# Layer 0's residual normalisation on other hooks, and the last norm's powers ahead of its pieces, in a two-layer decoder trunk on eight cores

## The chip, the cores and the metric

One Trainium2 chip, all eight NeuronCores. Each core runs the same program on its eighth of the tokens (two sequences of 4096 tokens, 8192 in all) and needs nothing from the others. The metric is device time in microseconds of the slowest core, the median of several runs.

Engines go by their profile names: PE is TensorE, DVE VectorE, ACT ScalarE, POOL GpSimd, SP SyncE, which here only issues DMAs.

## What is computed

The cut reference:

```python
x = layernorm(x, ln_in_g, ln_in_b)                 # the input norm, once
for l in range(2):
    h = x @ w_in[l] + b_in[l]                      # q k v gate_A u v_B gate_B route_A route_B
    y_a = window_attention(q, k, v, sinks[l]) * silu(gate_A)
    y_b = gelu(u) * (tril(W_s) @ layernorm(gelu(v_B)) + b_s) * silu(gate_B)
    m = sigmoid(route_A) * (y_a @ P_A[l]) + sigmoid(route_B) * (y_b @ P_B[l])
    x = layernorm(alpha * x + m @ W_out[l] + b_out[l], ln_g[l], ln_b[l])
```

The model width is 1024. Attention looks back 128 positions, the spatial gate mixes within chunks of 128.

## The kernel before, in words

Tokens are worked in tiles of 512, four blocks (j = 0 to 3) of 128. A stage is one tile in one layer. Stages come in fours: tiles 2i and 2i + 1 in layer 0, then both in layer 1, so that stage s is the first of a layer 0 pair for s % 4 = 0, the second for s % 4 = 1, and layer 1 for the rest; there are 32 (s = 0 to 31). A stage runs through these regions on PE: vb (four token-major tiles for v_B), u, gb and ga (four feature-major tiles each for u, gate B and gate A), r (sixteen tiles for the two routes, with the attention of the tile interleaved), pb (eight merge tiles with P_B, and the transposes of the next stage's input xbf into xT behind every second one), q of the next stage, pa (eight merge tiles with P_A), kv of the next stage, and then the output projection, which is emitted at the head of the next stage. All weights stream through four ring slots, one slab of 1 MB each; releasing a slab issues the load of the fourth one behind it on SP (the first uses of a slab go through POOL's queue from the float32 original, and a bf16 copy is written back by SP).

Dependences are found by the program `P.add` from keys such as ("xres", buf, j): an instruction waits for the last writer of what it reads, and for the readers of what it writes. Every engine runs its own instructions strictly in the order in which they were emitted, a DMA wait on SP included. What sets that order around the change are hooks: `run_hooks(hooks, ("u", 2))` stands behind the third u tile, and whatever was hooked there is emitted at that place, in the order of the `hook` calls. In the loop over stages (L915 to L954) the calls come in this order: third_hooks, lnin_hooks, lnin_before, resid_hooks, and region_out with its own hooks.

- `resid_hooks` (L672) works for layer 0 on the residual of the tile. The input x is loaded again into xres (`load`, a 512 KB DMA on SP), normalised by ACT (`app`, L680, an activation 128x1024), and multiplied and added to by POOL (`ln_gb`, L445, four instructions 128x512 per block). xres has two buffers, by tile parity. It is needed as late as the output projection.
- `third_hooks` (L545) multiplies and adds, on POOL, the output of the stage before last, behind each block of the output projection; for layer 1 it also issues y's DMA on SP behind vb 0, vb 1, vb 2 and u 0. The buffer is the one which the residual loads of the same stage write.
- `lnin_hooks` (L666) serves a stage before a layer 0 stage: statistics of the next tile's input blocks 2 and 3, which sit in stg, then an activation of each into xbf (`apply`). xbf is read by the transposes in pb. `ln_rstd` (L428) takes a power on POOL, `ln_bias` (L435) a small product on DVE.
- `region_mid` (L693): ACT evicts every u, gb and ga tile from PSUM; DVE multiplies uT by gbT, makes `mixed` from PSUM, and multiplies it by uT into gbT. PE's tiles take their PSUM buffer from a pool: five for these tiles ("W"), three for the scores ("S"), three for the route tiles ("A").
- `region_attn` (L762): scores (j, c) are masked by DVE (L777), their maximum taken (L780), then ACT's exponentials write Pq; POOL divides by the denominator (`norm`); `turn` transposes, `pv` multiplies.
- `region_pa` (L874): each merge tile has a product on DVE from PSUM, and a sum tRb <- tRa + tRb on DVE.
- `final_out` (L560) is the output projection of the last stage. Per block DVE adds the product, takes statistics and POOL the power f1. `finish(j)` scales on ACT, then has two POOL pieces and a DMA per half; `centre` and `scale` do the same work with two DVE instructions per half.

Of the kernel before, what the change touches and what calls it, by code (L numbers as in the profile page):

```python
# [151 lines left out]
def build(n_tok, seq_len):  # L152
# [50 lines left out]
    gb = sb("gb", [128, 6, D])  # L203
# [356 lines left out]
    def final_out(s):  # L560
# [7 lines left out]
            c = slice(h * 512, (h + 1) * 512)  # L568
            dma(eng, y_d[r0:r0 + 128, c], xres[:, buf, j, c], (("yh", j, h),), (("y", t, j, h),), ("yf", j, h))

        def finish(j, hs=(0, 1)):
            key = ("xres", buf, j)
            stt(sm[k][:, 2, j:j + 1], mv[k][:, j, 0:1], -1.0, ALU.mult, sm[k][:, 1, j:j + 1], ALU.mult,
                (("mv", k, j), ("f1", j)), (("f2", j),))
            for h in hs:
                c = slice(h * 512, (h + 1) * 512)
                d, hk = xres[:, buf, j, c], ("yh", j, h)
                act(d, d, AF.Identity, (key, ("f1", j), ("f2", j)), (hk,), bias=sm[k][:, 2, j:j + 1],
                    scale=sm[k][:, 1, j:j + 1])
                tt("pool", d, d, gb[:, gi, c], ALU.mult, (hk, ("gb", gi)), (hk,))  # L580
                tt("pool", d, d, gb[:, gi + 1, c], ALU.add, (hk, ("gb", gi + 1)), (hk,))
                put(j, h)
# [14 lines left out]
        for j in range(4):  # L597
            key = ("xres", buf, j)
            x = xres[:, buf, j, :]
            for h in range(2):  # L600
                b = next_bank("W")
                sl = slab8(so[h])
                for kc in range(8):
                    mm(ps[b][:], tRb[:, kc, j * 128:(j + 1) * 128], sl[:, kc, :], kc == 0, kc == 7,
                       RK(so[h]) + (("tRb", kc),), (("ps", b),))
                z = xres[:, buf, j, h * 512:(h + 1) * 512]
                stt(z, z, 2.0 * ALPHA, ALU.mult, ps[b][:], ALU.add, (key, ("ps", b)), (key,))
                P.add("dve", (lambda z, j, h: lambda e: e.bn_stats(out=st[:, j, 6 * h:6 * h + 6], in_=z))(z, j, h),
                      (key,), (("st", j) if h == 0 else ("st2", j),))
            P.add("dve", (lambda j: lambda e: e.bn_aggr(out=mv[k][:, j, :], in_=st[:, j, :]))(j),  # L610
                  (("st", j), ("st2", j)), (("mv", k, j),))
            ts("dve", sm[k][:, 0, j:j + 1], mv[k][:, j, 1:2], 4.0 * EPS, ALU.add, (("mv", k, j),), (("f0", j),))
            tt("pool", sm[k][:, 1, j:j + 1], sm[k][:, 0, j:j + 1], neghalf[:, 0:1], ALU.pow,
               (("f0", j), ("neghalf",)), (("f1", j),))
            if j in (1, 2):
                finish(j - 1)
        finish(2, (0,))
        centre(3, 0)
        centre(3, 1)
        scale(3, 0)  # L620
        scale(3, 1, "act")
        centre(2, 1)
        scale(2, 1)
        release(2)

    def hook(hooks, k, f):
# [36 lines left out]
        hook(hooks, ("pa", 3), lambda: apply(1))  # L663
        hook(hooks, ("pa", 6), lambda: (load(2), load(3)))

    def lnin_hooks(s, hooks):  # L666
        load, stats, apply = lnin_parts(s)
        hook(hooks, ("vb", 1), lambda: stats(2))
        hook(hooks, ("u", 2), lambda: apply(2))
        hook(hooks, ("u", 3), lambda: apply(3))  # L670

    def resid_hooks(s, hooks):  # L672
        t, l = stages[s]
# [10 lines left out]
        if s == 0:  # L684
            at = (("r", 15), ("pb", 1), ("pb", 3), ("pb", 5))
        else:
            at = (("gb", 1), ("gb", 3), ("ga", 1), ("pb", 1))
        for j in range(4):
            if s > 0:
                hook(hooks, (("u", 1), ("u", 2), ("u", 3), ("gb", 0))[j], (lambda j: lambda: load(j))(j))  # L690
            hook(hooks, at[j], (lambda j: lambda: (app(j), ln_gb(buf, j, 0)))(j))

    def region_mid(s, hooks):  # L693
# [221 lines left out]
    for s in range(NS):  # L915
# [16 lines left out]
            third_hooks(s - 1, hooks, (("gb", 0), ("gb", 2), ("ga", 0), ("ga", 2)),  # L932
                        (("ga", 0), ("ga", 2), ("r", 0), ("r", 2)))
        if is_lnin(s):
            lnin_hooks(s, hooks)
        if is_lnin(s + 1):
            lnin_before(s + 1, hooks)
        if stages[s][1] == 0:
# [92 lines left out]
```

How the kernel before makes its waits and increments, by code:

```python
        def run(ename, e):  # L99
            seen = {}
            for op in per_eng[ename]:
                waits = {}
                for d in op.deps:
                    if d.chan is None and d.eng == "pe" and ename == "pe" and op.chan is None:
                        continue
                    s, v = event(d)
                    if v > waits.get(s, (None, 0))[1]:
                        waits[s] = (s, v)
                if op.chan is not None and not self.chan_batch[op.chan] and op.ticket > 1:
                    s = csem[op.chan]
                    v = 16 * (op.ticket - 1)
                    if v > waits.get(s, (None, 0))[1]:
                        waits[s] = (s, v)
                for s, v in waits.values():
                    if seen.get(s, 0) < v:
                        e.wait_ge(s, v)
                        seen[s] = v
                ins = op.fn(e)
                if op.chan is not None:
                    ins.then_inc(csem[op.chan], 16)
                elif op.signal:
                    ins.then_inc(esem[ename], 1)
            if ename == "sp":
                for c, s in csem.items():
                    v = 16 * self.chan_count[c]
                    if seen.get(s, 0) < v:
                        e.wait_ge(s, v)
                        seen[s] = v
```

## Time and profile before

| | |
|---|---|
| median of 3 runs | 3605.0 us (3602.7 to 3606.3) |
| the profiled execution | 3604.8 us |
| its span, slowest core (core 3) | 3603.3 us |
| spans of the eight cores | 3575.7 to 3603.3 us |
| PE busy | 3410.5 us (95%) |
| DVE busy | 2318.8 us (64%) |
| ACT busy | 1824.2 us (51%) |
| POOL busy | 1401.2 us (39%) |
| chain that ended last: PE | 87% |
| chain: DMA, DVE, ACT | 6%, 3%, 1% |
| granted PE clock, core 3, mean | 0.982 |

The span is cut into stages of 103 to 130 us behind the first one. The busy time of an engine is the union of its instructions. Behind an instruction of a timeline the brackets give the time in which its engine was idle just before it, and what ended that idleness; x4 means that four like instructions were merged into the line, whose length then runs from the first one's start to the last one's end. Matmuls overlap, so the start of the next tells more than the length of one. The granted clock is the share of TensorE's full 2.4 GHz that it was given: 1.00, or 0.50 for the 1.2 GHz level.

### The profile page before, as it was taken

To read this page: it belongs to the slowest core of one execution; us is meant where nothing else is said; L and a number is where in the kernel's file an instruction comes from. 1 tells how busy PE (TensorE), PEld (TensorE's weight loads), DVE (VectorE), ACT (ScalarE), POOL (GpSimd) and SP (SyncE) were. 2 spreads that over 40 slices of the span, in tenths; PEclk is the share of its full clock that TensorE was granted. 3 is DMA by queue.
4 is the path that set the end of the run, shared out by engine and by line. 5 is a ranking of instruction groups with operands and counts; after the bars stand their busy time and mean duration, and the time that the engine had idled before them with its cause. 6 is when DMAs were issued, how large, how long until landed. Compare 5 with 4: busy or idle time off the path is not lost.

```text
span 3603.3 us, 61737 instructions; the slowest of 8 cores (3575.7 to 3603.3 us)
## 1 busy us (share of the span) xinstructions
PE 3410.5 (95%) x18320; PEld 1600.3 (44%) x18320; DVE 2318.8 (64%) x4993; ACT 1824.2 (51%) x4065; POOL 1401.2 (39%) x1295
## 2 busy tenths in 40 slices
PE   5778989999999999999999999999999999999997
PEld 2334444444444444444444444444444444444443
DVE  3445557666676676676776666766666667666667
ACT  3434445545555545655445654455654554555543
POOL 1324135442355331543334523444325542254343
PEclk9889999999999999999999999999999999999999
DMA  8784975538355344454454444544445534455433
GB/s 164 170 234 99 184 198 193 181 112 228 135 199 182 135 158 147 170 188 143 159 174 144 178 150 164 193 148 148 145 158 199 182 135 155 138 182 187 144 133 112
DMA packets 99112, 589.84 MB, mean 164 GB/s; under 512 B 11234, under 2 KB 11490, under 8 KB 42212
## 3 DMA queue, kind: packets, MB, share of 16 engines
q1 hardware_dynamic: 91012, 536.13, 42.2%
q0 software_dynamic: 7056, 49.29, 8.4%
q8 instruction: 159, 2.61, 0.3%
q14 instruction: 165, 1.35, 0.1%
q10 hardware_dynamic: 720, 0.46, 0.0%
HBM read 573.25 MB, written 61.87 MB: 176 GB/s over the span
## 4 chain that ended last, share of the span: by engine, by line
PE 87%; DMA 6%; DVE 3%; issue 1%; ACT 1%; POOL 0%; SPq 0%; DVEq 0%; POOLq 0%; ACTq 0%
PE ps L247 84%; DMA ring<-wpk 3%; PE ps L459 2%; PE ps L813 2%; DMA stg<-x 1%; DMA xres<-x 1%; DVE gbT L258 1%; ACT xT L255 1%; DMA tRb<-bs 1%; DVE nmx L780 0%; DVE ps L777 0%; DVE tRa L268 0%; DVE sm_i L268 0%; ACT L787 0%; POOL xres L258 0%
## 5 line engine op out<-in xcount | busy, mean ns | idle before, releaser
L247 PE MATMUL ps<-xT,ring 128*128 128x512 bf16 x8448 | 1967.7, 382 | 44.4 <-DMA ring<-wpk 25.0
L247 PEld LDWEIGHTS ps<-xT,ring 128*128 128x128 bf16 x8448 | 822.1, 98 | 1024.8 <-issue 105.5
L258 POOL TENSOR_TENSOR xres<-xres,gb 128x512 f32<-128x512 f32 x762 | 988.1, 1300 | 223.4 <-ACT xres L255 141.4
L258 POOL TENSOR_TENSOR Pq<-Pq,rcp 128x512 bf16<-128x512 bf16 x256 | 261.3, 1041 | 1010.2 <-DVE rcp L800 808.7
L787 ACT ACTIVATE Pq<-ps,nmx 128x128 bf16<-128x128 f32 x1024 | 371.8, 375 | 322.3 <-DVE nmx L268 320.3
L247 PE MATMUL ps<-ring,tRb 128*128 128x512 bf16 x2048 | 452.1, 381 | 19.0 <-DMA ring<-wpk 17.3
L247 PEld LDWEIGHTS ps<-ring,tRb 128*128 128x128 bf16 x2048 | 199.6, 98 | 257.9 <-issue 29.7
L247 PE MATMUL ps<-ring,xT 128*128 128x512 bf16 (+1 forms) x2048 | 304.3, 299 | 0.0
L255 ACT ACTIVATE xres<-xres,sm_p 128x1024 f32<-128x1024 f32 (+1 forms) x129 | 155.7, 1220 | 253.6 <-DVE sm_p L268 250.3
L258 POOL TENSOR_TENSOR sm_p<-sm_p,neghalf 128x2 f32<-128x2 f32 (+1 forms) x66 | 45.6, 691 | 577.9 <-DVE sm_p L262 574.8
L247 PE MATMUL ps<-gbT,ring 128*128 128x512 bf16 x1024 | 257.2, 379 | 0.0
L780 DVE TENSOR_REDUCE nmx<-ps 128x2 f32<-128x256 f32 x512 | 217.5, 425 | 54.6 <-DVE ps L777 2.3
L268 DVE SCALAR_TENSOR_TENSOR tRa<-tRa,ps 128x512 bf16<-128x512 bf16 x256 | 174.3, 681 | 120.8 <-PE ps L247 120.7
L247 PE MATMUL ps<-gaT,ring 128*128 128x512 bf16 x1024 | 230.5, 381 | 16.0 <-DVE tRa L268 14.5
L268 DVE SCALAR_TENSOR_TENSOR xres<-xres,ps 128x512 f32<-128x512 f32 x256 | 174.9, 683 | 99.2 <-PE ps L247 93.6
L247 PE MATMUL ps<-kpad,qT 128*128 128x512 bf16 x512 | 196.3, 383 | 39.5 <-DVE nmx L780 22.2
L258 DVE TENSOR_TENSOR uT<-uT,gbT 128x512 bf16<-128x512 bf16 x128 | 81.7, 649 | 225.2 <-ACT gbT L255 225.2
L255 ACT ACTIVATE xT<-ps,cs 128x512 bf16<-128x512 bf16 x256 | 186.1, 782 | 78.6 <-PE ps L459 74.9
L777 DVE COPY_PREDICATED ps<-upper,ps 128x256 f32<-128x256 uint16 x496 | 208.2, 420 | 18.2 <-PE ps L247 18.0
L255 ACT ACTIVATE xbf<-xres,sm_p 128x1024 bf16<-128x1024 f32 x64 | 79.2, 1238 | 276.3 <-DVE sm_p L268 276.3
L247 PEld LDWEIGHTS ps<-ring,xT 128*128 128x128 bf16 x2048 | 160.1, 98 | 128.2
L787 ACT ACTIVATION_READ_ACCUMULATOR Pq<-ps,nmx 128x1 f32 x1024 | 217.0, 212 | 0.0
(92 smaller groups left out, 3619.4 us busy)
## 6 DMA issues: line engine op xcount, KB each, us to landing
ring<-ws SPq DMA_DIRECT2D x371, 1024.0 KB, 5.8
ring<-wpk POOLq DMA_DIRECT2D x45, 1024.0 KB, 13.8
xres<-x SPq DMA_DIRECT2D x64, 512.0 KB, 6.8
stg<-x SPq DMA_DIRECT2D x60, 512.0 KB, 6.2
y<-xres SPq DMA_DIRECT2D x60, 512.0 KB, 4.8
ws<-ring SPq DMA_DIRECT2D x26, 1024.0 KB, 12.1
ring<-ws SPq DMA_DIRECT2D x28, 512.0 KB, 4.4
gb<-gbr SPq DMA_DIRECT2D x6, 512.0 KB, 13.6
```

What stands on the lines that cost most here:

```text
L247: P.add("pe", lambda e: e.matmul(out, lhsT, rhs, start=start, stop=stop), reads, writes)
L255: P.add("act", lambda e: e.activation(out=out, in_=in_, func=func, **kw), reads, writes)
L258: P.add(eng, lambda e: e.tensor_tensor(out=out, in0=in0, in1=in1, op=op), reads, writes)
L268: P.add("dve", lambda e: e.scalar_tensor_tensor(out=out, in0=in0, scalar=s, in1=in1, op0=op0, op1=op1), reads, writes)
L459: P.add("pe", (lambda o, i: lambda e: e.transpose(out=o, in_=i, identity=ident_bf[:]))(o, i), (("xbf", j), ("ident",)), (("ps", BX),))
L777: P.add("dve", lambda e: e.copy_predicated(out=o[:, :, 1, :], mask=upper[:].bitcast(mybir.dt.uint16).rearrange("p (h k) -> p h k", h=2), d ...
L780: P.add("dve", lambda e: e.tensor_reduce(out=nmx[:, q, 2 * c:2 * c + 2], in_=o[:, :, 1, :], axis=mybir.AxisListType.X, op=ALU.max, negate= ...
L787: P.add("act", (lambda hk: lambda e: e.activation(out=Pq[:, q, hk * 4 + c, :], in_=o[:, hk, 1, :], func=AF.Exp, scale=0.125, bias=nmx[:, q ...
L813: P.add("pe", (lambda h: lambda e: e.transpose(out=psP[:, h * 128:(h + 1) * 128], in_=Pq[:, q, h, :], identity=ident_bf[:]))(h), (("Pq", q ...
```

## The change

Nothing that is computed changes, nor how often. Work of layer 0's residual moves to other hooks: the four loads one hook earlier for every s > 0; for s > 1 the activation and the four POOL instructions of block 0 from (gb, 1) to (u, 2), of block 1 from (gb, 3) to (gb, 0), of block 2 from (ga, 1) to (r, 15), of block 3 from (pb, 1) to (pb, 3). Stage 1 keeps the old places of these. Where the stage is layer 0 and the next one too (s = 4, 8, ..., 28), lnin_hooks' two activations move from (u, 2) and (u, 3) to (gb, 2) and (ga, 0). In final_out, block 1's `finish` is emitted behind the power of block 3 instead of ahead of it, and the first half of block 2 goes from `finish` (ACT, POOL) to `centre` and `scale` (DVE), behind block 3's.

```diff
@@ -568,11 +568,11 @@
             c = slice(h * 512, (h + 1) * 512)
             dma(eng, y_d[r0:r0 + 128, c], xres[:, buf, j, c], (("yh", j, h),), (("y", t, j, h),), ("yf", j, h))
 
-        def finish(j, hs=(0, 1)):
+        def finish(j):
             key = ("xres", buf, j)
             stt(sm[k][:, 2, j:j + 1], mv[k][:, j, 0:1], -1.0, ALU.mult, sm[k][:, 1, j:j + 1], ALU.mult,
                 (("mv", k, j), ("f1", j)), (("f2", j),))
-            for h in hs:
+            for h in range(2):
                 c = slice(h * 512, (h + 1) * 512)
                 d, hk = xres[:, buf, j, c], ("yh", j, h)
                 act(d, d, AF.Identity, (key, ("f1", j), ("f2", j)), (hk,), bias=sm[k][:, 2, j:j + 1],
@@ -612,15 +612,16 @@
             ts("dve", sm[k][:, 0, j:j + 1], mv[k][:, j, 1:2], 4.0 * EPS, ALU.add, (("mv", k, j),), (("f0", j),))
             tt("pool", sm[k][:, 1, j:j + 1], sm[k][:, 0, j:j + 1], neghalf[:, 0:1], ALU.pow,
                (("f0", j), ("neghalf",)), (("f1", j),))
-            if j in (1, 2):
-                finish(j - 1)
-        finish(2, (0,))
+            if j == 1:
+                finish(0)
+        finish(1)
         centre(3, 0)
         centre(3, 1)
         scale(3, 0)
         scale(3, 1, "act")
-        centre(2, 1)
-        scale(2, 1)
+        for h in range(2):
+            centre(2, h)
+            scale(2, h)
         release(2)
 
     def hook(hooks, k, f):
@@ -663,11 +664,11 @@
         hook(hooks, ("pa", 3), lambda: apply(1))
         hook(hooks, ("pa", 6), lambda: (load(2), load(3)))
 
-    def lnin_hooks(s, hooks):
+    def lnin_hooks(s, hooks, at=(("vb", 1), ("u", 2), ("u", 3))):
         load, stats, apply = lnin_parts(s)
-        hook(hooks, ("vb", 1), lambda: stats(2))
-        hook(hooks, ("u", 2), lambda: apply(2))
-        hook(hooks, ("u", 3), lambda: apply(3))
+        hook(hooks, at[0], lambda: stats(2))
+        hook(hooks, at[1], lambda: apply(2))
+        hook(hooks, at[2], lambda: apply(3))
 
     def resid_hooks(s, hooks):
         t, l = stages[s]
@@ -684,10 +685,10 @@
         if s == 0:
             at = (("r", 15), ("pb", 1), ("pb", 3), ("pb", 5))
         else:
-            at = (("gb", 1), ("gb", 3), ("ga", 1), ("pb", 1))
+            at = (("u", 2), ("gb", 0), ("r", 15), ("pb", 3)) if s > 1 else (("gb", 1), ("gb", 3), ("ga", 1), ("pb", 1))
         for j in range(4):
             if s > 0:
-                hook(hooks, (("u", 1), ("u", 2), ("u", 3), ("gb", 0))[j], (lambda j: lambda: load(j))(j))
+                hook(hooks, (("vb", 2), ("u", 1), ("u", 2), ("u", 3))[j], (lambda j: lambda: load(j))(j))
             hook(hooks, at[j], (lambda j: lambda: (app(j), ln_gb(buf, j, 0)))(j))
 
     def region_mid(s, hooks):
@@ -932,7 +933,10 @@
             third_hooks(s - 1, hooks, (("gb", 0), ("gb", 2), ("ga", 0), ("ga", 2)),
                         (("ga", 0), ("ga", 2), ("r", 0), ("r", 2)))
         if is_lnin(s):
-            lnin_hooks(s, hooks)
+            if stages[s][1] == 0 and s > 0:
+                lnin_hooks(s, hooks, (("vb", 1), ("gb", 2), ("ga", 0)))
+            else:
+                lnin_hooks(s, hooks)
         if is_lnin(s + 1):
             lnin_before(s + 1, hooks)
         if stages[s][1] == 0:
```

## Rows read from the trace of the kernel before

**Rows 1.** windows, six stages from 4 to 30: stretch, length, busy by engine

```profile
582.30:691.20 108.90, 105.27 (x573) 49.68 (x572) 72.11 (x156) 56.40 (x127) 53.58 (x47) 1.00 0.48 169
...
1014.50:1124.70 110.20, 106.84 (x573) 50.02 (x572) 72.33 (x156) 56.97 (x128) 53.92 (x48) 0.98 0.49 168
...
1124.70:1231.60 106.90, 105.36 (x574) 49.73 (x573) 70.71 (x148) 58.99 (x130) 53.04 (x47) 1.00 0.48 173
...
3164.50:3274.90 110.40, 106.89 (x573) 50.03 (x572) 72.41 (x156) 56.86 (x128) 53.90 (x48) 0.98 0.48 167
...
3274.90:3382.10 107.20, 105.33 (x573) 49.72 (x572) 70.71 (x148) 59.06 (x130) 52.99 (x47) 1.00 0.48 173
...
3382.10:3487.30 105.20, 105.14 (x574) 49.68 (x573) 65.86 (x148) 54.67 (x126) 31.62 (x31) 1.00 0.39 136
```

**Rows 2.** waits of PE, 560 to 3460 us: total, times, longest

```profile
PE ps L247 <- DVE nmx L780: 20.7, 7, 3.6
...
PE ps L247 <- ACT Pq L787: 10.2, 6, 3.3
```

**Rows 3.** timeline, stage 8 (last line 9): start, length, instruction, [idle before]

```profile
1031.72 1.24 ACT L255 ACTIVATE xbf<-stg,sm_i 128x1024 bf16<-128x1024 f32 x1 [3.29 <-DVE sm_i L268]
...
1039.65 17.91 POOL L258 TENSOR_TENSOR xres<-xres,gb 128x512 f32<-128x512 f32 x12 [9.20 <-ACT xres L255]
...
1040.19 2.43 DVE L258 TENSOR_TENSOR uT<-uT,gbT 128x512 bf16<-128x512 bf16 x2 [1.28 <-ACT gbT L255]
...
1047.06 2.50 DVE L258 TENSOR_TENSOR gbT<-mixed,uT 128x512 bf16<-128x512 f32 x2
...
1049.48 0.42 DVE L777 COPY_PREDICATED ps<-upper,ps 128x256 f32<-128x256 uint16 x1
...
1053.13 0.59 PE L247 MATMUL ps<-kpad,qT 128*128 128x512 bf16 x1 [3.22 <-DVE nmx L780]
...
1161.42 0.38 PE L247 MATMUL ps<-kpad,qT 128*128 128x512 bf16 x1 [1.31 <-ACT Pq L787]
```

**Rows 4.** timeline, layer 1 stage 10, first masked score

```profile
1263.11 0.42 DVE L777 COPY_PREDICATED ps<-upper,ps 128x256 f32<-128x256 uint16 x1
```

**Rows 5.** window behind the wait in stage 8; PEclk is the granted clock

```profile
1053.10:1056.50 3.40, 3.37 (x8) 1.12 (x9) 2.46 (x5) 3.17 (x12) 2.97 (x4) 0.50 0.01 2
```

**Rows 6.** SP timeline, stage 8; then xres DMAs of SP, 560 to 3400

```profile
1015.25 7.51 SPq L278 DMA_DIRECT2D y<-xres  x3
...
DMA to landing us min/median/max: 3.0/6.7/10.0
```

**Rows 7.** timeline, P_B of stage 9

```profile
1191.79 1.46 ACT L255 ACTIVATE xT<-ps,cs 128x512 bf16<-128x512 bf16 x2
...
1193.12 1.26 ACT L255 ACTIVATE xres<-xres,sm_i 128x1024 f32<-128x1024 f32 x1
...
1193.39 0.61 PE L459 MATMUL ps<-ident_bf,xbf 128*128 128x128 bf16 x8
```

**Rows 8.** timeline: POOL in stage 8, then P_A of layer 1 stage 10

```profile
1095.79 5.49 POOL L258 TENSOR_TENSOR xres<-xres,gb 128x512 f32<-128x512 f32 x4
...
1314.45 1.44 DVE L258 TENSOR_TENSOR tRb<-tRa,tRb 128x512 bf16<-128x512 bf16 x1
...
1319.19 1.02 PE L247 MATMUL ps<-gaT,ring 128*128 128x512 bf16 x4 [0.46 <-DVE tRa L268]
```

**Rows 9.** timeline, stage 1

```profile
245.45 1.24 ACT L255 ACTIVATE xres<-xres,sm_i 128x1024 f32<-128x1024 f32 x1 [14.56 <-DMA xres<-x]
...
247.41 3.57 PE L247 MATMUL ps<-xT,ring 128*128 128x512 bf16 x8 [9.22 <-ACT gbT L255]
```

**Rows 10.** timeline of the end

```profile
3594.42 0.55 POOL L258 TENSOR_TENSOR sm_p<-sm_p,neghalf 128x1 f32<-128x1 f32 x1
...
3595.14 3.27 DVE L268 SCALAR_TENSOR_TENSOR xres<-xres,sm_p,gb 128x512 f32<-128x512 f32 x2 [3.20 <-POOL sm_p L258]
...
3599.18 0.75 DVE L268 SCALAR_TENSOR_TENSOR xres<-xres,sm_p,gb 128x512 f32<-128x512 f32 x1
```

## The prediction, made before the changed kernel had run

> **What bounds the kernel now.** I read the page first: TensorE is busy for 95% of the span and holds 87% of the chain that ended last, so a microsecond counts only where TensorE waits, runs at the lower clock, or has finished. So I cut the trace at the first bias-row matmul of each stage and asked for the busy time of each stretch [rows 1]. A stage in which TensorE waits for nothing takes 105.2 us (stage 30, the last row). Behind stage 1 there are fourteen layer 0 stages, of two kinds: the first of a pair takes 108.9 us in stage 4 and 110.2 to 110.4 us in the six from stage 8 to 28; the second (5, 9, ..., 29) 106.9 to 107.2 us from stage 9 on.
>
> The list of waits names the cause [rows 2]: in the steady part TensorE waits 20.7 + 10.2 us in 13 places for the scores' maxima (nmx) or for Pq. By stage, that is one wait of 3.1 to 3.6 us in each of the seven first stages, and 0.9 to 1.6 us (mean 1.34) in each of the seven second ones, always where the gate tiles end and the attention begins; the timeline of stage 8 shows how the long one comes about [rows 3]. ScalarE stands 3.29 us for the input norm's statistics, then evicts late. VectorE needs 2.43 us for two uT products and 2.50 us for two gbT products, while GpSimd runs twelve xres pieces without a break (17.91 us). So VectorE reaches the first masked score at 1049.48, 34.9 us into the stage, and TensorE, whose next score matmul needs a buffer freed, stands for 3.22 us. In the layer 1 stage 10, which began at 1231.6 and where GpSimd is idle at this point, the first masked score comes at 1263.11, 31.5 us in [rows 4], and TensorE does not wait. Stage 9, a second one, lies between with 1.31 us [rows 3]. Right behind the wait of 3.22 us the granted clock is 0.50, the 1.2 GHz level, for 3.4 us with TensorE busy [rows 5]: 1.7 us lost, on this core in the six first stages from 8 on.
>
> **The change part by part.** The residual's work on one block is a load, one activation on ScalarE (1.24 us) and four pieces on GpSimd (1.37 us each, 5.49 us for four [rows 8]). All of it stays; it moves.
>
> *Gate to attention, first stages.* Blocks 0 and 1 go to the hooks (u, 2) and (gb, 0), 2 and 3 to (r, 15) and (pb, 3). GpSimd then has 8 x 1.37 = 11 us of pieces from about +17 to +28 us in the stage, instead of twelve pieces from +25 to +43. Besides, lnin's two activations leave (u, 2) and (u, 3), so ScalarE no longer stands for their statistics. Laid out with the durations of rows 3, ScalarE evicts uT(3) at +17 (now +18.3) and has caught up by gaT(1), and VectorE comes to the first score at +31.6 to +32, as in layer 1. Of the wait of 3.3 us (mean of the six) I leave 0.2: -3.1, and with it goes the fall of the clock, -1.6. In stage 4, where the clock did not fall, -3.2. In second stages ScalarE has one to_bf and one second step between the same hooks, so of 1.34 us I leave 0.3: -1.0. How much stays is the unknown; the bounds are 0 and the 1.3 of a second stage today.
>
> *Loads.* They move one hook up, to (vb, 2), (u, 1), (u, 2), (u, 3). Block 0's load goes out on SP ahead of the weight slab that is requested when the vb slab is released, and has to wait until y(0) of the same buffer has landed; y(0) to y(2) leave SP between 1015.25 and 1022.76 [rows 6]. I put the load at +9.3 us and the slab behind it 1.3 us later than now; that slab is needed three slabs later, some 20 us, so this costs nothing. Outputs and residual loads take 3.0 to 10.0 us from issue to landing, 6.7 in the median [rows 6]: block 0 lands at +12 to +19, and ScalarE wants it at +14; since it stands until +17 today, no loss. Loads 1 to 3 leave about when 0 to 2 do now, behind y(3).
>
> *P_B.* Here the change costs. The activation of block 2 gets ahead of the evictions of the first xbf transposes. Today, in stage 9, these evictions start at 1191.79 and take 1.46 us, and TensorE's next transposes start at 1193.39, 0.14 us behind their end [rows 7]: there is no slack. With an activation of 1.26 us ahead (1.14 net of overlap) they come 1.1 us later, and TensorE stands for it. The activation of block 3, now two merge tiles later, finds ScalarE idle between evictions, and the small wait that it causes today (0.14) goes: +1.0 us net in each of 14 stages. From below, 0, if something else hides it; from above, both activations are waited out, 2.3.
>
> *P_A.* GpSimd's queue holds eight pieces behind (r, 15) where it held four; the output pieces behind them, which run from 1095.79 for 5.49 us and end just as P_A's products begin, slide some 5 us into P_A. Stage 10 shows what this does [rows 8]: one tRb sum takes 1.44 us, and later TensorE waits 0.46. There a small statistics step is stretched as well; here two or three sums collide and nothing else, so I take 0.2 us, between 0 and 1.0.
>
> A page of the Trainium skill bears on this, SBUF — State Buffer, section "SBUF: two separate sides": a VectorE operation with two SBUF inputs and a GpSimd operation that reads SBUF exclude each other for a whole instruction. The trace agrees in kind: the uT, gbT and tRb operations that stretch have two SBUF inputs each [rows 3, 8].
>
> *Stage 1.* Only its loads move. ScalarE stands 14.56 us there for block 0's load, and TensorE 9.22 us for ScalarE [rows 9]. The load leaves 3 us earlier, ahead of a weight slab and two rows of constants. Then blocks 1 and 2 end the waits, they too some 3 us sooner: -3, between 0 and -9.
>
> *The end.* The power of block 3 runs at 3594.42, behind four pieces of block 1, and VectorE stands 3.20 us for it, from 3591.94 [rows 10]. Ahead of the pieces it is done by then. VectorE takes all of block 2 in exchange, so six operations follow 3591.94 where four follow 3595.14: two of block 3 and one more beside GpSimd at 3.27 / 2 = 1.64 us, three at 0.75, end at 3599.1 instead of 3599.93. With the step that block 3's chain no longer has ahead of it I take -1.0, between +1 and -3.
>
> The sum: six first stages (-3.1 - 1.6 + 1.0 + 0.2) x 6 = -21.0; stage 4 -3.2 + 1.2 = -2.0; seven second stages (-1.0 + 1.2) x 7 = +1.4; stage 1 -3; the end -1.0. Together -25.6 us. The profiled execution took 3604.8 us (its span 3603.3), the median of the runs is 3605.0, so nothing is corrected: **3579 us**.
>
> **The rivals.**
> *A: the gate wait stays in part and P_B costs more.* ScalarE now has block 1's activation and lnin's two in the same gate tiles, so VectorE stays late: 1.3 us left in first stages (clock back at full), 1.0 in second ones, 1.4 us at P_B, 0.6 in P_A. First stages -2.0 - 1.6 + 2.0 = -1.6, x 6; stage 4 about 0; second -0.3 + 2.0 = +1.7, x 7; stage 1 -3: about -1, 3604 us. For it: first and second stages differ mainly in ScalarE's load. Against it: stage 10, and that GpSimd is off VectorE's late steps.
> *B: slower.* Block 0's load lands late, and ScalarE, which works in order, stands at (u, 2) with the u and gate evictions behind it. TensorE has five buffers there; its first gate A tile, at about +22, needs the one of uT(3). From a landing at +20, 10.7 us behind the issue, each further microsecond costs one in each of 14 stages. To turn -26 into +9 it takes 2.5 us, a landing 13 us behind the issue: 3614 us. Against it: the longest of 112 is 10.0 [rows 6]; for it: the stand of 14.56 us in stage 1.
> *C: more.* P_B's delay is mostly absorbed (0.2 instead of 1.0 in 14 stages, -11) and stage 1 gives 7 (-4): -41, 3564 us.
> *D: VectorE and GpSimd exclude each other in full.* In P_A four sums lose 1 us each, and 0.9 us of it reaches TensorE: +0.7 x 14 = +10. At the end four operations cost 0.75 + 1.27 us each, which ends it at 3601.5: +1.6 instead of -1.0. Together -13, 3592 us. That is the case of the Trainium skill's rule in SBUF — State Buffer, section "SBUF: two separate sides", taken at its word.
>
> **How the numbers follow.** The forecast has 0.50, D 0.15, A 0.15, C 0.14, B 0.06. The range, 3563 to 3604, leaves out B and the outer halves of A and C, two in ten at most. A measurement of this kernel can tell 0.2% (7.2 us) from no change. Faster by more (below 3597.8): forecast, C, D and a little of A, 0.80; within: most of A, 0.14; slower: B, 0.06.
>
> **What would show it.** In first stages the wait behind nmx under 0.5 us, granted clock 1.00, the stage at about 106.8 us. At P_B a new wait of xbf transposes for xT of about 1 us in 14 stages. tRb sums of over 1 us at the head of P_A. In stage 1 ScalarE's first wait for xres at least 3 us shorter. At the end the power ahead of block 1's pieces. The prediction is wrong if the wait for nmx stays over 1 us, if xT costs under 0.3 or over 2 us, or if ScalarE stands for a load in steady stages.

## The result: slower by 0.7%, outside the range

Four runs of each kernel on one chip: the changed kernel took 3628.8 us in the median (3626.4 to 3630.6), the kernel before 3603.9 (3602.2 to 3606.3). The ratio is 1.0068, with a 95% interval of 1.0051 to 1.0086. The forecast was 3579 us with a range of 3563 to 3604: wrong in sign. All medians and ratios here leave out the executions, of any of the kernels, in which the cores of one die showed a lower granted clock and took some per cent longer.

The page of the changed kernel, its first line, the busy times and the chain:

```profile
span 3626.9 us, 61732 instructions; the slowest of 8 cores (3588.5 to 3626.9 us)
...
PE 3416.5 (94%) x18320; PEld 1600.6 (44%) x18320; DVE 2297.5 (63%) x4994; ACT 1822.9 (50%) x4064; POOL 1381.2 (38%) x1293
...
PE 86%; DMA 6%; DVE 4%; ACT 2%; issue 2%; SPq 0%; DVEq 0%; POOL 0%; ACTq 0%; POOLq 0%
```

The profiled execution took 3628.4 us, 23.6 more than the one of before. No engine has more work; VectorE is 21 us less busy, which I read as fewer of its products stretched by GpSimd's pieces. What grew is what TensorE does not do: the chain now goes 4% through VectorE and 2% through ScalarE.

The stages, cut in the same way as [rows 1] (stretch, length, busy time of PE, PEld, DVE, ACT and POOL, granted clock, DMA share, GB/s): stages 4, 8, 9, 10 and 29.

```profile
580.30:692.90 112.60, 107.11 (x573) 50.12 (x572) 71.01 (x156) 56.69 (x127) 52.11 (x47) 0.98 0.47 165
...
1017.30:1129.80 112.50, 107.13 (x573) 50.08 (x572) 71.24 (x156) 56.92 (x128) 52.42 (x48) 0.98 0.47 164
1129.80:1240.00 110.20, 107.05 (x574) 50.04 (x573) 67.90 (x148) 59.34 (x130) 52.17 (x47) 0.98 0.47 167
1240.00:1346.00 106.00, 105.34 (x573) 49.53 (x572) 70.75 (x156) 56.88 (x128) 32.16 (x32) 1.00 0.43 154
...
3297.20:3406.00 108.80, 105.41 (x566) 49.31 (x565) 68.04 (x145) 58.77 (x129) 50.24 (x46) 0.98 0.48 169
```

The layer 1 stages did not move (106.0 us here, 106.6 in the mean of the thirteen, before and after). All of the loss is in layer 0: the seven first stages take 111.9 us in the mean (110.1 before), the seven second ones 109.1 (106.9 before). The list of TensorE's waits (waited for: total, times, longest) from 560 to 3480 us, for [rows 2]:

```profile
PE ps L459 <- ACT xT L255: 17.1, 19, 1.6
PE ps L247 <- DVE nmx L268: 15.8, 10, 2.1
PE ps L247 <- DVE mixed L268: 15.4, 10, 2.4
PE ps L247 <- ACT Pq L788: 8.8, 5, 2.1
```

Two lines of the same list of before, 560 to 3460 us, that [rows 2] leave out:

```profile
PE ps L459 <- ACT xT L255: 1.1, 3, 0.4
...
PE ps L247 <- DVE nmx L268: 1.8, 2, 1.6
```

The 32.7 us of before for nmx and Pq (20.7, 10.2 and 1.8) have become 24.6, but 15.4 us for `mixed` and 17.1 for xT stand beside them, where before had none for mixed and 1.1 for xT. Of the growth of 27.6 us between the starts of stages 4 and 31 (2905.0 to 2932.6), the waits and the clock give 25.4; the other 2.2 stay unassigned:

| part, stages 4 to 30 | before | after | difference |
|---|---|---|---|
| gate to attention, seven first stages | 23.2 | 26.7 | +3.5 |
| gate to attention, seven second stages | 9.4 | 14.0 | +4.6 |
| P_B, xT, all fourteen (0.14 and 1.14 us a stage) | 2.0 | 15.9 | +13.9 |
| half of the time at clock 0.50 (20.5 and 30.7 us) | 10.2 | 15.3 | +5.1 |
| all other waits | 13.1 | 11.4 | -1.7 |

The list leaves out waits under 0.15 us, and with them the 0.14 us at P_B of before. Stage 4 begins 2.0 us sooner, which is not the change's: the slowest core is another one (core 5 instead of 3), and core 5 itself began it at 577.6 us before and at 580.3 now. The end behind the start of stage 31 is 1.9 us shorter (116.0 to 114.1): 27.6 - 2.0 - 1.9 = 23.7 us, the difference of the two spans but for rounding. The slowest core is typical: in the mean of the eight cores the stretch from stage 4 to 31 grew from 2904.7 to 2928.0 us.

**How the gate wait comes about now.** The timeline of stage 8, which begins at 1017.3 (start, length, instruction, [idle before]), for [rows 3]:

```profile
1026.54 0.34 SPq L278 DMA_DIRECT2D xres<-x  x1
...
1031.79 5.89 SPq L278 DMA_DIRECT2D xres<-x  x3
...
1033.08 1.24 ACT L255 ACTIVATE xres<-xres,sm_i 128x1024 f32<-128x1024 f32 x1 [1.90 <-DMA xres<-x]
...
1034.47 10.97 POOL L258 TENSOR_TENSOR xres<-xres,gb 128x512 f32<-128x512 f32 x8 [1.27 <-ACT xres L255]
...
1038.55 1.24 ACT L255 ACTIVATE xres<-xres,sm_i 128x1024 f32<-128x1024 f32 x1 [1.66 <-DMA xres<-x]
...
1040.83 1.24 ACT L255 ACTIVATE gbT<-ps,cs 128x512 bf16<-128x512 f32 x2
...
1041.60 2.71 DVE L258 TENSOR_TENSOR uT<-uT,gbT 128x512 bf16<-128x512 bf16 x2 [4.17 <-ACT gbT L255]
1044.24 1.22 DVE L268 SCALAR_TENSOR_TENSOR sm_i<-mv_i,sm_i 128x2 f32<-128x2 f32 x1
...
1045.55 1.24 ACT L255 ACTIVATE xbf<-stg,sm_i 128x1024 bf16<-128x1024 f32 x1 [3.47 <-DVE sm_i L268]
1046.69 0.67 ACT L255 ACTIVATE gbT<-ps,cs 128x512 bf16<-128x512 f32 x1
...
1047.46 0.43 DVE L258 TENSOR_TENSOR uT<-uT,gbT 128x512 bf16<-128x512 bf16 x1 [2.01 <-ACT gbT L255]
...
1048.70 0.38 PE L247 MATMUL ps<-wTbf,vnh 128*128 128x128 bf16 x4 [2.09 <-DVE mixed L268]
...
1053.37 0.42 DVE L778 COPY_PREDICATED ps<-upper,ps 128x256 f32<-128x256 uint16 x1
...
1057.02 0.38 PE L247 MATMUL ps<-kpad,qT 128*128 128x512 bf16 x1 [2.10 <-ACT Pq L788]
```

Read it in the order of time. ScalarE stands 1.90 us for block 0's load and 1.66 us for block 1's (issued +14.5 us into the stage, landed +21.2). So gbT(1) and gbT(2) are evicted only from 1040.83, and VectorE, idle for 4.17 us, gets its uT products at 1041.60. Behind these in its queue stands lnin's bias product, which (gb, 2) emits; beside GpSimd's pieces the two products take 2.71 us and the bias 1.22: it ends at 1045.46, just as the run of pieces does (1034.47 + 10.97 = 1045.44). ScalarE stands 3.47 us for it, and only then evicts gbT(3), for which VectorE stands 2.01 us. A ring: VectorE waits for ScalarE, which waits for VectorE, which waited for ScalarE. TensorE loses 2.09 us for the buffers of `mixed` and 2.10 us at the scores; the first masked score is 36.1 us into the stage, where it was 34.9. The clock falls behind it as it did before [rows 5]:

```profile
1058.30:1061.70 3.40, 3.40 (x10) 1.22 (x8) 0.70 (x5) 2.98 (x12) 0.00 (x0) 0.50 0.25 34
```

A second stage such as 9 has no lnin, so no ring; its loads land as late (block 1 +20.5 to +22.2), and its wait is 2.00 us in the mean where it was 1.34.

### The profile page after: what moved, and what is told of

It is laid out like the page before. It is cut to its first block, busy times and chain, and to the rows that moved or that the text cites. A ratio compares the mean times of both kernels' runs of the same rounds, so it can differ in the third digit from the quotient of the medians.

```text
span 3626.9 us, 61732 instructions; the slowest of 8 cores (3588.5 to 3626.9 us)
## 1 busy us (share of the span) xinstructions
PE 3416.5 (94%) x18320; PEld 1600.6 (44%) x18320; DVE 2297.5 (63%) x4994; ACT 1822.9 (50%) x4064; POOL 1381.2 (38%) x1293
## 4 chain that ended last, share of the span: by engine, by line
PE 86%; DMA 6%; DVE 4%; ACT 2%; issue 2%; SPq 0%; DVEq 0%; POOL 0%; ACTq 0%; POOLq 0%
PE ps L247 83%; DMA ring<-wpk 3%; PE ps L459 2%; PE ps L814 2%; DMA stg<-x 1%; DMA xres<-x 1%; ACT xT L255 1%; DMA tRb<-bs 1%; DVE nmx L781 0%; ACT xres L255 0%; DVE ps L778 0%; DVE tRa L268 0%; DVE sm_i L268 0%; DVE gbT L258 0%; DVE xres L268 0%
## 5 line engine op out<-in xcount | busy, mean ns | idle before, releaser
L258 POOL TENSOR_TENSOR xres<-xres,gb 128x512 f32<-128x512 f32 x760 | 967.8, 1277 | 133.7 <-ACT xres L255 51.9
L247 PE MATMUL ps<-ring,tRb 128*128 128x512 bf16 x2048 | 451.4, 381 | 17.0 <-DMA ring<-wpk 15.4
L268 DVE SCALAR_TENSOR_TENSOR tRa<-tRa,ps 128x512 bf16<-128x512 bf16 x256 | 174.2, 680 | 121.2 <-PE ps L247 121.0
L247 PE MATMUL ps<-gaT,ring 128*128 128x512 bf16 x1024 | 230.4, 381 | 15.9 <-DVE tRa L268 14.4
L258 DVE TENSOR_TENSOR uT<-uT,gbT 128x512 bf16<-128x512 bf16 x128 | 90.6, 720 | 239.1 <-ACT gbT L255 238.7
L268 DVE SCALAR_TENSOR_TENSOR xres<-xres,ps 128x512 f32<-128x512 f32 x256 | 175.0, 683 | 95.4 <-PE ps L247 90.0
```

What stands on the lines that cost most here:

```text
L247: P.add("pe", lambda e: e.matmul(out, lhsT, rhs, start=start, stop=stop), reads, writes)
L258: P.add(eng, lambda e: e.tensor_tensor(out=out, in0=in0, in1=in1, op=op), reads, writes)
L268: P.add("dve", lambda e: e.scalar_tensor_tensor(out=out, in0=in0, scalar=s, in1=in1, op0=op0, op1=op1), reads, writes)
```

## The experiments

The edits are against the changed kernel ("after") or against the kernel before, as said. "First" and "second" are the kinds of layer 0 stages; times within a stage count from its start. The kernel before, run beside each group of experiments, took 3604 to 3613 us in the median from group to group; ratios are against the runs of the same group.

### The end alone

Before, with the new final_out and nothing else.

> The kernel before with only the new order of the last output projection. Theory and rivals agree: from the first bias-row matmul of stage 31 to the end 114.1 us instead of 116.0, every other stage as before; about 3602 us. If the gain at the end hung on the state in which stage 31 is entered, it would be under 1 us here.

Measured: ratio 0.9990 (0.9979 to 1.0000); from the start of stage 31 the end takes 114.3 us instead of 116.0. The new order (the power ahead of block 1's pieces, and all of block 2 on VectorE) is worth 1.7 us.

### Blocks 0 and 1 early, 2 and 3 at their old places

```diff
-            at = (("u", 2), ("gb", 0), ("r", 15), ("pb", 3)) if s > 1 else ...
+            at = (("u", 2), ("gb", 0), ("ga", 1), ("pb", 1)) if s > 1 else ...
```

> The changed kernel with blocks 2 and 3 back at (ga, 1) and (pb, 1). Theory (ScalarE stands in the gate tiles, for the residual loads of blocks 0 and 1 and for lnin's bias, and P_B costs 1.07 us a stage by itself): the wait of xbf transposes for xT falls from 1.07 to 0.14 us in 14 stages, -13 us, and ScalarE's 1.26 us more at (ga, 1) gives back up to half; 3616 to 3622 us, first stages still with their wait for mixed of 1 to 3 us. Rival (the GpSimd pieces beside the uT and gbT products are the cause): twelve pieces in a row again, the gate waits grow by 2 us or more in each of 14 stages, 3630 us or above.

Measured: ratio 1.0120 (1.0102 to 1.0138), some 3651 us. P_B's wait is back at the 0.13 to 0.14 us a stage of before, so the place of blocks 2 and 3 was its cause, but the gate wait grows to 5.2 us in first stages and 4.0 in second ones, with 58 us at the low clock on the slowest core. Its waits of TensorE:

```profile
PE ps L247 <- DVE nmx L268: 28.0, 9, 3.8
PE ps L247 <- DVE mixed L268: 19.8, 10, 3.3
```

A third residual activation and twelve GpSimd pieces in the gate tiles cost more than P_B's delay. My number was missed by 30 us, and the time is the rival's (3630 or above). The run moves the activation and the pieces together, so it does not say which of the two adds the wait.

### Blocks 2 and 3 alone

Before, with blocks 2 and 3 at (r, 15) and (pb, 3).

> The kernel before with only blocks 2 and 3 moved to (r, 15) and (pb, 3) for s > 1. Theory: +1.0 us a stage at P_B (+14), and the gate wait falls from 3.3 to about 2.3 us in first and from 1.3 to about 0.5 us in second stages, as ScalarE has one activation less and GpSimd four pieces less there, with less time at the lower clock: -14 to -20; 3598 to 3606 us. Rival (nothing is gained at the gate by this): 3618 us.

Measured: ratio 1.0032 (1.0020 to 1.0043), some 3620 us. P_B costs 1.12 to 1.15 us in every stage; the gate waits stay at 3.31 and 1.24. So taking four pieces off GpSimd's run of twelve gains nothing by itself, and the rival held:

```profile
PE ps L247 <- DVE nmx L780: 21.5, 8, 3.4
PE ps L459 <- ACT xT L255: 17.1, 19, 1.6
```

### The bias product ahead of the uT products

After, with lnin's bias product emitted at (u, 2), ahead of the uT products; the activations stay at (gb, 2) and (ga, 0).

```diff
...
+        early = at[1] == ("gb", 2)
         hook(hooks, at[0], lambda: stats(2))
-        hook(hooks, at[1], lambda: apply(2))
+        if early:
+            hook(hooks, ("u", 2), lambda: ln_bias("i%d" % (stages[s + 1][0] % 2), 2))
+        hook(hooks, at[1], lambda: apply(2, not early))
```

> The changed kernel with lnin's bias product (0.16 us on VectorE) emitted at (u, 2), ahead of the uT products, while its activations stay at (gb, 2) and (ga, 0). Theory (ScalarE and VectorE wait for each other in a ring: gbT evictions behind the activation, the activation behind the bias, the bias behind the uT products): ScalarE's stand of 3.5 us before xbf goes, the wait for mixed (1.1 to 2.9 us) goes in all seven first stages, and first stages come to 108.5 to 110 us, like second ones; -15 to -22, 3607 to 3614 us. Rival (pieces beside products): the wait for mixed stays over 1 us, 3624 us or above.

Measured: ratio 1.0012 (1.0002 to 1.0022), median 3613 us: 0.68% of loss has become 0.12%, so 15 to 20 us of the 25 are back. In stage 8 the product now takes 0.15 us, and the waits of TensorE are:

```profile
1033.45 0.15 DVE L268 SCALAR_TENSOR_TENSOR sm_i<-mv_i,sm_i 128x2 f32<-128x2 f32 x1
...
PE ps L247 <- DVE nmx L268: 20.1, 12, 2.3
...
PE ps L247 <- DVE mixed L268: 6.3, 9, 1.1
```

First stages wait 2.4 us at the gate instead of 3.8 and take 109.8 us on this core, 108.2 on the best. In the mean of the eight cores the stretch from stage 4 to 31 takes 2911.0 us, 17 less than after. Of the 15.4 us for `mixed`, which I had expected to go, 6.3 are left. The ring was real, and it was not all.

### No residual loads of blocks 0 and 1

The kernel of the last experiment, with the loads of blocks 0 and 1 left out for s > 1 (their activations and pieces work on what the buffer holds).

> The kernel with the early bias, without the residual's loads of blocks 0 and 1 for s > 1 (what they would bring is left out of the result; their activations and pieces stay). Theory (what is left of the gate wait is ScalarE standing for these loads): ScalarE never stands for xres behind u 2 and gb 0, the gate wait falls from 1.9 to 2.4 us in first and 1.2 to 2.4 us in second stages to 0.3 to 0.7 us in both, and no longer varies from stage to stage; first stages 107.0, second 107.2 us, with 1.07 us at P_B. Rival (pieces beside products): the gate wait stays at 1.5 us or more.

Measured, in one run: 3577.1 us. No gate wait is left in first stages (106.4 us), 0.30 in second ones, 3.4 us at the low clock. So the wait needs the late landings. With the loads out of the way the same order gives just the stages that the forecast had promised, although all GpSimd pieces are still there.

```profile
PE ps L247 <- DVE nmx L268: 1.6, 5, 0.7
```

### No GpSimd pieces of blocks 0 and 1

The same kernel with the loads, but without the eight pieces of blocks 0 and 1 for s > 1.

> The kernel with the early bias, without GpSimd's four pieces each of blocks 0 and 1 for s > 1 (their scale and shift are left out of the result; loads and activations stay). Theory (ScalarE's stands make most of what is left): the gate wait falls by 0.5 to 1.2 us, since the uT products no longer stretch (2.3 to 2.7 us for two becomes 0.9), and 0.7 to 1.2 us stay, with the scatter between stages. Rival (pieces beside products are the cause): it falls to under 0.2 us in both kinds of stage.

Measured, in one run: 3584.6 us; gate wait 1.0 to 1.7 us by core in first stages (mean 1.34, with the pieces 2.15) and 0.05 to 0.4 in second ones (0.23, with them 1.80), though ScalarE stands for the loads about as long (for blocks 0 and 1, in first stages, 2.04 and 2.53 us; 2.45 and 1.83 with the pieces). Half a miss: I had expected the loads alone to hold the wait. The pieces, which stretch the products behind the late evictions, are worth 0.8 us of it in first stages and nearly all of it in second ones; there taking away either of the two is enough.

### lnin's activations back at (u, 2) and (u, 3)

> The changed kernel with lnin's hooks where they were, (u, 2) and (u, 3). Theory (the ring of waits needs the bias behind the uT products): the wait for mixed goes here too, since the bias is then ahead of all uT products; ScalarE has two activations more ahead of the gate evictions, which are 2.4 us later than in the changed kernel, so the wait for nmx grows to 3 to 4 us in first stages; these take 110 to 112 us, second ones as in the changed kernel. Rival: the wait for mixed stays over 1 us.

Measured, in one run: 3626.4 us, 13 above the kernel before beside it, where after was 25 above; gate waits 3.03 and 2.20. From stage 4 to 31 the cores take 2924.2 us in the mean, where after takes 2928.0 and before 2904.7. ScalarE no longer stands for a load in first stages, since its activation of block 0 comes only at +18.4, but it has two xbf activations ahead of the evictions. So the move of lnin cost some 4 us of the 23 as it was made. It has two parts that nearly cancel: the bias product behind the uT products costs 17 us (2928.0 against 2911.0), and with that product early the move of the activations gains 13 (2924.2 against 2911.0).

### lnin still earlier, residual at its old places

Before, with the new end, the statistics at (vb, 0) and lnin's activations at (vb, 3) and (u, 0) in first stages, and the last pieces of the stage before last moved on by one hook to make room.

```diff
-        hook(hooks, ("vb", 1), lambda: stats(2))
-        hook(hooks, ("u", 2), lambda: apply(2))
-        hook(hooks, ("u", 3), lambda: apply(3))
+        at = (("vb", 0), ("vb", 3), ("u", 0)) if s > 0 and stages[s][1] == 0 else (("vb", 1), ("u", 2), ("u", 3))
+        hook(hooks, at[0], lambda: stats(2))
+        hook(hooks, at[1], lambda: apply(2))
+        hook(hooks, at[2], lambda: apply(3))
```

> The kernel before with the new end, and in the first stages of a layer 0 pair lnin's statistics at (vb, 0), its activations at (vb, 3) and (u, 0), and the output pieces of block 3 behind them at (vb, 1); the residual stays at (gb, 1), (gb, 3), (ga, 1), (pb, 1). Theory (ScalarE's stand of 3.3 us for lnin's statistics, and its two activations in the u and gate tiles, make the long gate wait): ScalarE evicts u and gate tiles in step, the gate wait of first stages falls from 3.3 to 0.5 to 1.3 us, their low clock goes, they take 106 to 107 us; second stages stay at 106.9; 3575 to 3585 us. Rival (the twelve GpSimd pieces beside the gbT products make it): the wait stays at 2.5 us or more, 3600 us.

Measured: 3590.3 us, ratio 0.9936 (0.9917 to 0.9956): faster than before. First stages take 108.2 us with a gate wait of 2.2 (expected 0.5 to 1.3: missed). ScalarE's stand has moved with the activations, to 13.4 us into the stage (4.77 us), where little is queued behind it:

```profile
1028.57 1.24 ACT L255 ACTIVATE xbf<-stg,sm_i 128x1024 bf16<-128x1024 f32 x1 [4.77 <-DVE sm_i L268]
```

What the edit moves besides: in first stages the residual loads go out later, block 0's at +16.7 us where it was +14.5.

### Both put together, with hooks chosen by the landings

The kernel of the last experiment, with the loads at the new places, and the residual at hooks at which its data is there: (u, 3), (gb, 1), and (pb, 1), (pb, 5) instead of (r, 15), (pb, 3).

```diff
-            at = (("gb", 1), ("gb", 3), ("ga", 1), ("pb", 1))
+            at = (("u", 3), ("gb", 1), ("pb", 1), ("pb", 5)) if s > 1 else (("gb", 1), ("gb", 3), ("ga", 1), ("pb", 1))
...
-                hook(hooks, (("u", 1), ("u", 2), ("u", 3), ("gb", 0))[j], (lambda j: lambda: load(j))(j))
+                hook(hooks, (("vb", 2), ("u", 1), ("u", 2), ("u", 3))[j], (lambda j: lambda: load(j))(j))
```

> The kernel with lnin early and the new end, and for s > 1 the residual's loads at (vb, 2), (u, 1), (u, 2), (u, 3) as in the change, but its work one tile later than there, at (u, 3) and (gb, 1), and for blocks 2 and 3 at (pb, 1) and (pb, 5). Theory (the change fails because ScalarE comes to its loads before they land, and by its place at P_B): the loads land at about +16 and +21 to +22 and ScalarE comes to them at +17 and +22, so its stands are under 0.5 us; the pieces end before the last gbT products; gate wait 0.3 to 0.9 us in both kinds of stage, P_B 0.2 to 0.4 us, low clock near 0; layer 0 stages 106.2 to 106.8 us; 3572 to 3580 us. Rival (the earlier residual work is wrong at any place in u and gb): gate wait over 1.5 us, above 3590 us.

> The same kernel as e9_combined, timed again beside e11_bias_vb1 and the kernel before, since only two undisturbed runs of it are known (3577.9 and 3581.0). Both theories of e11_bias_vb1: 3577 to 3582, faster than the kernel before by 0.6 to 0.8%; first stages 107.2 to 107.9 with a gate wait of 1.5 to 2.1, second stages 105.5 to 105.8.

Measured: two runs in the first group, 3577.9 and 3581.0 us; six in the second, median 3569.7 (3567.5 to 3578.9), ratio 0.9885 (0.9858 to 0.9911). That is some 1.1% faster than the kernel before, more than the 0.6 to 0.8% expected. P_B's wait is back at 0.13 to 0.15 us, and second stages wait 0 to 0.6 at the gate. First stages wait 1.6 to 1.9 us there, where 0.3 to 0.9 was expected, and take 107.1 to 107.7 us by core. Stages 8 and 9 of its core 0, in windows as above, and its waits (core 6, 560 to 3440 us):

```profile
1007.80:1115.00 107.20, 105.28 (x573) 49.58 (x572) 72.42 (x156) 56.30 (x128) 53.55 (x48) 1.00 0.50 172
1115.00:1220.40 105.40, 105.21 (x574) 49.80 (x573) 68.37 (x148) 58.94 (x130) 52.88 (x47) 1.00 0.50 176
...
PE ps L247 <- DVE nmx L268: 7.4, 6, 1.7
PE ps L247 <- DVE nmx L782: 5.2, 3, 1.8
```

Block 0's activation starts at +18.9 in first stages with the data there since +15.2, block 1's at +23.8 (landed +21.9): no stand there (in second ones up to 1.6 us for block 1). The parts that cost 0.3 and 1.2% by themselves are in it, at other hooks, and the whole gives 38 us against the 3608.1 of the kernel before in the same group.

### P_B's places in the changed kernel

The kernel with the early bias product, with blocks 2 and 3 at (pb, 1) and (pb, 5).

> The kernel with the early bias, with blocks 2 and 3 at (pb, 1) and (pb, 5) instead of (r, 15) and (pb, 3). Theory (at (r, 15) the activation stands ahead of the first xT evictions, which have no slack; behind the second tile ScalarE has some): the wait for xT falls from 1.14 to 0.1 to 0.3 us a stage, the gate waits stay at 1.2 to 2.4 us; -12 us against the early bias alone, about 3596 us. Rival (an activation costs TensorE 1 us wherever it stands in P_B): the sum of the waits in P_B stays at 1 us.

Measured: ratio 1.0003 (0.9985 to 1.0022), some 3609 us. The wait at P_B is nearly what it was before (0.15 to 0.20 us a stage), which should give 13 us against the early bias product alone, but only 3 to 4 came (0.12% of loss has become 0.03%). The gate waits grew instead: in the mean of the eight cores from 2.15 to 2.44 us in first stages and from 1.80 to 2.25 in second ones, and in first stages block 1's load lands at +21.3 to +22.3 on the mean of a core where it was +20.9 to +21.9. Later landings would do this; why they are later no run isolates.

```profile
PE ps L459 <- ACT xT L255: 1.9, 6, 0.4
```

### The bias product at (vb, 1)

The combined kernel, with the bias product behind the statistics at (vb, 1).

> e9_combined with one more change in the first stages: lnin's bias product of blocks 2 and 3 is emitted on VectorE at (vb, 1), right behind the statistics, not at (vb, 3) behind v_B's statistics and products. In e9_combined ScalarE still stood 4.77 us for it in first stages, until 13.4 us into the stage, and TensorE waited 1.55 to 2.07 us at the gate (second stages 0.1 to 0.3). Theory (what is left of the first stages' wait is this stand): ScalarE is free by +10, has its evictions done in time, the gate wait of first stages is at most 0.5 us, their length 105.5 to 106.3, the time 3565 to 3573. Rival (the wait comes from the 12 GpSimd pieces stretching VectorE's products, as e6_no_pieces hinted, not from ScalarE's order): first stages stay at 107 to 108 with a wait of 1.5 to 2.1, the time within 3 us of e9_combined's 3578 to 3581.

Measured: first stages 106.3 to 106.9 us by core with a gate wait of 0.6 to 1.3 (combined: 107.2 and 1.6), so the earlier product was worth some 0.6 us a stage and the other half of the expected gain is not there: about 1 us is left with ScalarE in time, as the run without pieces had hinted. The time is unclear: eight runs spread from 3562.5 to 3608.2 us, median 3573.8, ratio 0.9910 (0.9876 to 0.9943). In the profiled one two cores took 140 and 142 us for stage 1, which this edit does not touch, and the other six 124 to 132. Four runs (3562.5 to 3567.1) are below all of the combined kernel's; which of the two is faster stays open.

## Why the prediction was wrong

*What bounds the kernel.* Right: TensorE, and its waits in layer 0 at the change from gates to attention (one in each of fourteen stages; the text counts 13 places, since the 1.64 us of stage 29 stand under L268). Right too, the durations on which the sum stood.

*Gate to attention, first stages: the step that failed.* Forecast: 3.1 us of wait and 1.6 of clock gained in each. Measured: a wait longer by 0.5 and as many falls of the clock as before (six), with three elsewhere (stages 6, 9 and 29). The text laid ScalarE out: "evicts uT(3) at +17 (now +18.3) and has caught up by gaT(1)". uT(3) came at +16.9 as said. What failed lies behind it, in three places:

- *Block 1's load.* I laid the landing against ScalarE's wish for block 0 only. By my own numbers (issue at about +14.5, 6.7 us to the landing [rows 6]) block 1 lands at +21.2. ScalarE came to it at +19.6 in stage 8, as it does when the steps behind uT(3) at +17 are added up. It landed at +20.7 to +21.5 in first stages. The number was in the text, and the comparison was not made.
- *"Since it stands until +17 today, no loss."* The stand of before was for lnin's statistics, which the change moves away; I used it as cover for the load in the very kernel in which it is gone. Block 0 landed at +15.7, inside my +12 to +19, and ScalarE stood 1.9 us for it. Without both loads (and the bias product early) the wait is zero.
- *lnin's bias product.* The text moves "two activations". The hook emits a product on VectorE too, and at (gb, 2) three uT products are ahead of it. It takes 1.22 us where it takes 0.15 alone, and costs ScalarE 3.47 us. Emitting it early gave 15 to 20 us back. It had no term in the sum.

Of the signs named for a wrong prediction two came: the waits for nmx or Pq stay at some 2 us, and ScalarE stands for loads in steady stages.

*Second stages.* Forecast -1.0, measured +0.66 each, for the two first reasons: without the loads 0.30 is left, which is just the forecast.

*Clock.* Not gained since the waits stayed; 10.2 us more at 0.50 cost 5.1 us.

*P_B.* Right in place and size: +1.0 net of the 0.14 of before was forecast, and 0.14 became 1.14 (1.12 to 1.15 in the run with blocks 2 and 3 alone). The rows of stage 8 show the activation ahead of the xT evictions, and TensorE behind both:

```profile
1089.08 1.24 ACT L255 ACTIVATE xres<-xres,sm_i 128x1024 f32<-128x1024 f32 x1
1090.21 1.45 ACT L255 ACTIVATE xT<-ps,cs 128x512 bf16<-128x512 bf16 x2
...
1091.81 0.61 PE L459 MATMUL ps<-ident_bf,xbf 128*128 128x128 bf16 x8 [1.08 <-ACT xT L255]
```

*P_A.* Forecast +0.2, measured none. GpSimd's output pieces did slide by the forecast 5 us (1103.40 is 86.1 us into stage 8; 1095.79 was 81.3 [rows 8]), but only one tRb sum was stretched, to 0.70 us, and TensorE did not wait:

```profile
1103.40 5.67 POOL L258 TENSOR_TENSOR xres<-xres,gb 128x512 f32<-128x512 f32 x4
...
1108.65 0.70 DVE L258 TENSOR_TENSOR tRb<-tRa,tRb 128x512 bf16<-128x512 bf16 x1
```

*Stage 1.* Forecast -3, measured 0: 128.98 us in both. Its rows, for [rows 9]:

```profile
238.67 1.24 ACT L255 ACTIVATE xres<-xres,sm_i 128x1024 f32<-128x1024 f32 x1 [9.89 <-DMA xres<-x]
...
240.63 3.57 PE L247 MATMUL ps<-xT,ring 128*128 128x512 bf16 x8 [4.39 <-ACT gbT L255]
...
247.37 1.24 ACT L255 ACTIVATE xres<-xres,sm_i 128x1024 f32<-128x1024 f32 x1 [6.31 <-DMA xres<-x]
...
249.91 0.59 PE L247 MATMUL ps<-kpad,qT 128*128 128x512 bf16 x1 [5.28 <-ACT gaT L255]
254.07 1.24 ACT L255 ACTIVATE xres<-xres,sm_i 128x1024 f32<-128x1024 f32 x1 [4.30 <-DMA xres<-x]
```

Block 0's load left 1.8 us sooner and not 3 (+25.0 instead of +26.8), yet it was there 6.0 us sooner (+33.2 instead of +39.2), and its stand shrank from 14.56 to 9.89 us. But blocks 1 and 2 landed at +41.9 and +48.6, 1.8 sooner and 1.6 later than before, and the stands moved to them: TensorE's 9.22 us became 4.39 and 5.28. "They too some 3 us sooner" had no row behind it. The fourth landed at +51.1 in both. The four loads go out among weight slabs, and an earlier issue of the first did not bring the last; what held them up no run isolates.

*The end.* Forecast -1.0, measured -1.9 (-1.7 in the run of the end alone). Right in mechanism: the power of block 3 runs at 3614.01, ahead of block 1's pieces, and VectorE does not stand for it.

```profile
3614.01 1.08 POOL L258 TENSOR_TENSOR sm_p<-sm_p,neghalf 128x1 f32<-128x1 f32 x1 [0.55 <-DVE sm_p L268]
...
3613.93 1.42 DVE L268 SCALAR_TENSOR_TENSOR xres<-xres,mv_p,gb 128x512 f32<-128x512 f32 x2
3615.33 3.35 DVE L268 SCALAR_TENSOR_TENSOR xres<-xres,sm_p,gb 128x512 f32<-128x512 f32 x2
3618.61 1.74 DVE L268 SCALAR_TENSOR_TENSOR xres<-xres,mv_p,gb 128x512 f32<-128x512 f32 x1
3620.45 1.56 DVE L268 SCALAR_TENSOR_TENSOR xres<-xres,sm_p,gb 128x512 f32<-128x512 f32 x1
...
3622.78 0.75 DVE L268 SCALAR_TENSOR_TENSOR xres<-xres,sm_p,gb 128x512 f32<-128x512 f32 x1
```

From the end of the centring to VectorE's last instruction it takes 8.2 us (3615.35 to 3623.53), as long as before (8.0), where I had forecast 7.2: four instructions run beside GpSimd, at 1.56 to 1.74 us each, where I had put three at 1.64. The gain comes ahead of it, a term that I had put at 0.2 us: the centring itself (1.42 us for two, before 2.41 beside GpSimd), the small product ahead of it (0.16 instead of 0.86), and 0.4 us from an earlier start.

*The rivals.* B named the right mechanism, ScalarE standing for a load with the evictions behind it, and had a chance of 0.06. Its price was wrong in its threshold: it began to count at a landing of +20 for block 0, because it let TensorE's five buffers take up everything before, and it did not look at block 1. Measured, a landing of +15.7 and one of +21.2 were enough, since the delay adds up with the ring and the stretched products before it meets the buffers. A, ScalarE with too many activations in the gate tiles, had its sizes too small (1.3 and 1.0 us left at the gate; 3.8 and 2.0 were measured), and the difference of first and second stages, which it put down to ScalarE's load, is mostly the bias product: with that early and the same activations in place, they wait 2.15 and 1.80 us in the mean of the cores. C did not occur. D's full exclusion did not show: at the end four operations ran beside GpSimd, as D had it, but one took 1.56 to 1.74 us and not 2.0, and in P_A one sum of eight was stretched, by 0.28 us.

The Trainium skill's page SBUF — State Buffer, section "SBUF: two separate sides", has it that a VectorE operation with two SBUF inputs and a GpSimd operation that reads SBUF lock each other out for a whole instruction. The trace agrees where the prediction did not apply the rule, at the small product with two SBUF inputs: 0.15 us alone, 1.22 us beside pieces of 1.37 us, so what it pays is up to one piece, whatever its own size. I had looked for the rule's effect at large products alone.

## What to carry to other kernels

When a change removes what an in-order engine stands for, lay the arrival of everything else it needs against the new, earlier time, block by block; cover that the change itself takes away is no cover. Follow every instruction of a moved helper on every engine, the smallest too, and ask what stands ahead of it in that queue: a product of 0.15 us behind two others held ScalarE for 3.47 us. Test the parts of a reordering apart and together: here blocks 2 and 3 alone cost 0.3%, blocks 0 and 1 with the moved lnin 1.2%, all of it 0.7%, and the same loads with hooks matched to their landings and lnin earlier gained some 1.1% with the new end.

## What was not expected of the hardware

- A VectorE product of 128x2 elements takes 0.15 us alone and 1.22 us beside GpSimd's pieces; one of 128x1 at the end 0.16 and 0.86 us. It goes the other way too: GpSimd's power takes 0.54 to 0.56 us, and 1.08 beside VectorE's centring.
- The fall of the clock is not told by the length of one wait. On the slowest core of after, waits of 2.10, 2.06 and 2.14 us (stages 8, 9, 12) were followed by 3.4 us at 0.50, while 2.07 to 2.12 us (stages 13, 16, 17 and 25) were not.
- The eight cores, with the same program, differ in after by 26 us at the start of stage 4 (553.8 to 580.3 us) and by 17 us from there to stage 31 (2916 to 2933), and in it the two slowest cores are the two that start stage 4 last.
